# A hybrid decoder layer: own tokens scored as extra key columns, the first sample softmax between the prompt heads, a fused mask and maximum, stacked rotary scores

## The chip, the cores and the metric

One of the eight cores of a Trainium2 chip runs the whole kernel. A core has a matrix engine (TensorE, called PE in the profile), a vector engine (VectorE, DVE), a scalar engine for activations and copies (ScalarE, ACT), a general engine (GpSimd, POOL), and SyncE (SP), which here issues nearly all transfers to 16 DMA engines. They share the on-chip memory SBUF; PE writes its results to PSUM, eight banks of 512 fp32 numbers per partition. Each engine works through its own list of instructions in order and waits on semaphores for the others. The metric is the time of one execution in microseconds; lower is better.

## What is computed

One step of one decoder layer for a prompt of 256 tokens and for 8 sequences of 8 new tokens each, whose 1024 earlier tokens lie in a paged cache. In short:

```python
h = rmsnorm(x); z = h @ w_in                # q | latent c_kv | k_rope | pool input | 2 gates
# prompt: 16 heads, causal, 128 + 64 (rotary) dimensions
s = (q_nope @ k_nope.T + q_rope @ k_rope.T) * ATTN_SCALE
p = softmax(where(mask, s, -inf)); o = p @ v
# sample, per sequence: 1024 cached latents and 8 of its own tokens
q_lat = einsum('thd,rhd->thr', q_nope, w_uk)
s = (q_lat @ c_all.T + q_rope @ kr_all.T) * ATTN_SCALE     # 8 tokens x 16 heads = 128 rows
o_lat = softmax(where(mask, s, -inf)) @ c_all; o = o_lat @ w_uv
merged = sigmoid(gA) * (o @ w_attn_out) + sigmoid(gB) * (pooled @ w_pool_out)
x = x + merged @ w_o; x = x + conv_glu(rmsnorm(x)); y = rmsnorm(x)
```

Everything is fp32. The kernel gets near that precision with the faster format fp32r by splitting each operand in a high part (the value rounded to fp32r) and a low part (the rest), and adding high x high, high x low and low x high.

## The kernel before

The 320 tokens are the moving columns of nearly every product. The weights come in slabs of 128 x 2048 numbers (1 MB). For each slab SP issues the transfer into `w_raw`, ACT copies it to `w_hi` (L484), DVE subtracts to `w_lo` (L884) and PE forms the products (L1434); two buffers of each alternate. Every engine has its part of the program written out by hand, and semaphores with counted values tie them together (`hi_ready`, `lo_ready`, `slab_used`, `slab_taken`).

**Start.** ACT's own queue brings `vec` (the gains and other vectors) and the first tile of x (L549, L550); SP's queue brings the first slab in pieces and the other tiles of x.

**`uk` and `uv`.** Eight slabs give the keys `kT` and values `vv` of the prompt.

**Prompt heads.** A loop of 16 heads and three more steps. In step i, PE scores head i in fp32 (`qn` with `kT`, and for the rotary part `qr` with `kr_half`, a copy of the rotary key for even and odd heads in which the other half of the rows is zero), transposes the probabilities of head i - 2 (L1672) and applies those of head i - 3 to the values. DVE scales and masks the scores in one pass (L1185) and takes two row maxima (L1191, one per 128 queries), divides head i - 1 by its sum (L1196, L1200), and makes the low part of the output of head i - 4 (`o_lo`). ACT does the exponentials (L706), copies the turned probabilities (`pt`) and the outputs (`o_hi`). Between these stand the first pieces of the sample part: latent queries (PE steps 1 to 8), the splitting of the first cached pages into halves (ACT `w_hi`, `k_rope`; DVE `w_lo`, `k_rope`), and the scores of sequence 0 (PE steps 11 to 15) and the first of sequence 1 (step 17).

**Sample loop.** A sequence has two groups of four pages, q = 0 and 1. Its scores are two chunks of 512 columns in two PSUM banks, each of fourteen products: eight with the high keys, four with the low keys, two rotary. `new_scores` adds a third piece: the 8 x 8 = 64 own tokens of all sequences, in fp32, masked so that only the sequence's own 8 count. Then the maximum (DVE, L1240 to L1247), the exponentials (ACT, L749, L751), the division (DVE, L1258), the turn on PE (L1729, L1733), its copy to SBUF (`spt`), and the product with the token-major pages (`c_raw`). The order on PE for sequence i is: scores q = 0 of i, turn of i - 1, scores q = 1 of i, own scores of i, values of i - 1.

After this PE goes through the output projections and the feed-forward part, which the change leaves alone.

## Time and profile before

| | us |
|---|---|
| median of 3 runs | 1988.13 (1987.9 to 1988.9) |
| the profiled execution | 1988.56 |
| its span, first to last instruction | 1986.6 |
| PE busy | 1959.0 (99%) |
| DVE busy | 1092.2 (55%) |
| ACT busy | 761.2 (38%) |

The profile records one execution. PE is busy nearly throughout; a product shows a busy time longer than its distance from the next, since products overlap in the pipeline, so distances between starts are what a product costs. The granted clock of PE is 1.0 in almost every slice (1.0 is 2.4 GHz, 0.5 is 1.2 GHz). The sixteen heads run from 606 to about 671 us, the sample loop until 798.

### The profile page before, as it was taken

The page shows a single profiled execution, that of the slowest core. Times are in us where ns is not written, and L with a number is a line of the kernel's source. Part 1 is how long each engine was busy: PE and PEld are TensorE (multiplying, and loading weights), DVE is VectorE, ACT ScalarE, POOL GpSimd, SP SyncE. Part 2 cuts the span into 40 slices and gives each one's busy share as a digit, 9 for nine tenths or more (in the row PEclk, how much of TensorE's full clock was granted, in tenths as well). Part 3 has the DMA queues.
Part 4 walks back from the last instruction along what each step waited for, and adds up shares of the span by engine and source line. Part 5 has one row for each costly group of instructions (what it writes and reads, how often), then busy time and mean ns, then how long its engine had stood idle before and what let it go on. Part 6 is the DMA issues. An engine that isn't in the chain of part 4 may idle for free.

```text
span 1986.6 us, 33915 instructions
## 1 busy us (share of the span) xinstructions
PE 1959.0 (99%) x13368; PEld 1935.2 (97%) x13368; DVE 1092.2 (55%) x1469; ACT 761.2 (38%) x836; POOL 48.8 (2%) x188
## 2 busy tenths in 40 slices
PE   8999999999999899999999999999999999999997
PEld 8999999999998799999999999999999999999997
DVE  6865344333335764355556655555556555565656
ACT  5356542332246654233334232333323333333334
POOL 1002000000000000000000000000000000000000
PEclk9999999999999999999999999999999999999998
DMA  6444444444444487454444434344444444444443
GB/s 248 142 151 178 148 148 148 148 149 148 149 173 157 141 281 285 149 202 149 149 150 158 163 136 161 148 148 148 148 148 148 148 149 148 146 153 143 159 140 121
DMA packets 59878, 318.13 MB, mean 160 GB/s; under 512 B 6514, under 2 KB 6834, under 8 KB 27186
## 3 DMA queue, kind: packets, MB, share of 16 engines
q1 hardware_dynamic: 58882, 312.85, 44.5%
q10 hardware_dynamic: 944, 4.57, 0.6%
q8 instruction: 34, 0.56, 0.1%
q14 instruction: 18, 0.15, 0.0%
HBM read 313.08 MB, written 4.32 MB: 160 GB/s over the span
## 4 chain that ended last, share of the span: by engine, by line
PE 97%; DVE 1%; ACT 1%; DMA 1%; issue 0%; SPq 0%; DVEq 0%; ACTq 0%
PE ps L1434 96%; PE ps L1729 0%; DVE w_lo L884 0%; DMA xT<-in_x 0%; DVE y_gain L884 0%; DMA w_raw<-in_cache_t 0%; DVE neg_max L1191 0%; ACT w_hi L484 0%; DVE sm L1185 0%; ACT sm L706 0%; SPq L359 0%; DVE k_rope L884 0%; ACT qlat L484 0%; PE ps L1672 0%; ACT pt L484 0%
## 5 line engine op out<-in xcount | busy, mean ns | idle before, releaser
L884 DVE TENSOR_TENSOR w_lo<-w_raw,w_hi 128x2048 fp32r<-128x2048 f32 (+2 forms) x270 | 608.1, 2253 | 453.8 <-ACT w_hi L484 453.5
L1434 PE MATMUL ps<-h_hi,w_hi 128*128 128x320 f32 x2512 | 742.0, 308 | 9.1 <-ACT w_hi L484 9.1
L484 ACT ACTIVATE w_hi<-w_raw 128x2048 fp32r<-128x2048 f32 (+2 forms) x272 | 508.4, 1870 | 624.5 <-PE ps L1434 624.2
L1434 PE MATMUL ps<-h_lo,w_hi 128*128 128x320 f32 x2512 | 741.2, 309 | 0.0
L1434 PEld LDWEIGHTS ps<-h_hi,w_hi 128*128 128x128 f32 x2512 | 473.0, 188 | 9.6 <-ACT w_hi L484 9.1
L1434 PEld LDWEIGHTS ps<-h_lo,w_hi 128*128 128x128 f32 x2512 | 471.5, 188 | 0.5 <-DVE h_lo L985 0.3
L1434 PE MATMUL ps<-h_hi,w_lo 128*128 128x320 f32 x2496 | 391.1, 308 | 0.0
L1434 PEld LDWEIGHTS ps<-h_hi,w_lo 128*128 128x128 f32 x2496 | 372.5, 187 | 0.0
L1434 PE MATMUL ps<-hid_hi,w_hi 128*128 128x320 f32 x704 | 216.5, 308 | 0.0
L1434 PE MATMUL ps<-hid_lo,w_hi 128*128 128x320 f32 x704 | 216.5, 308 | 0.0
L1434 PE MATMUL ps<-hid_hi,w_lo 128*128 128x320 f32 x704 | 216.5, 307 | 0.0
L1434 PEld LDWEIGHTS ps<-hid_hi,w_hi 128*128 128x128 f32 x704 | 131.9, 187 | 0.0
L1434 PEld LDWEIGHTS ps<-hid_lo,w_hi 128*128 128x128 f32 x704 | 131.9, 187 | 0.0
L1434 PEld LDWEIGHTS ps<-hid_hi,w_lo 128*128 128x128 f32 x704 | 131.9, 187 | 0.0
L868 ACT ACTIVATE silu<-cv,vec 128x336 f32<-128x336 f32 x44 | 25.4, 577 | 213.0 <-DVE cv L1380 213.0
L884 DVE TENSOR_TENSOR x<-ps,x 128x320 f32<-128x320 f32 x176 | 80.3, 486 | 47.1 <-PE ps L1434 47.1
L1434 PE MATMUL ps<-o_hi,w_hi 128*128 128x320 f32 x256 | 75.4, 307 | 0.0
L1434 PE MATMUL ps<-o_lo,w_hi 128*128 128x320 f32 x256 | 75.3, 308 | 0.0
L1434 PE MATMUL ps<-m_lo,w_hi 128*128 128x320 f32 x256 | 75.3, 308 | 0.0
L1434 PE MATMUL ps<-m_hi,w_hi 128*128 128x320 f32 x256 | 75.3, 307 | 0.0
L1380 DVE SCALAR_TENSOR_TENSOR cv<-aext,vec,cv 128x336 f32<-128x336 f32 x88 | 50.1, 569 | 11.0 <-DVE cv L1377 0.2
L1434 PE MATMUL ps<-spt,c_raw 128*128 128x128 f32 x448 | 51.9, 276 | 0.0
(230 smaller groups left out, 1766.7 us busy)
## 6 DMA issues: line engine op xcount, KB each, us to landing
w_raw<-in_slabs SPq DMA_DIRECT2D x253, 1024.0 KB, 4.8
w_raw<-in_cache_t SPq DMA_DIRECT2D x64, 288.0 KB, 4.1
c_raw<-in_cache SPq DMA_DIRECT2D x56, 256.0 KB, 4.8
w_whole<-in_slabs SPq DMA_DIRECT2D x4, 1024.0 KB, 7.0
x_again<-in_x ACTq DMA_DIRECT2D x1, 2560.0 KB, 9.8
c_last<-in_cache SPq DMA_DIRECT2D x8, 256.0 KB, 4.2
xT<-in_x SPq DMA_DIRECT2D x3, 640.0 KB, 8.6
out_y<-y_gain SPq DMA_DIRECT2D x2, 640.0 KB, 3.1
```

Source lines behind the costliest of these rows:

```text
L484: return nc.scalar.activation(out, in_, ACT.Copy)
L868: nc.scalar.activation(silu[:, f % 2, CW - 1:], cv[:, 2, CW - 1:], ACT.Silu, bias=vec[:, bass.ds(c * FPC + (VEC["conv_b"] + f), 1)]).then_ ...
L884: return nc.vector.tensor_tensor(out, a, b, op)
L1380: nc.vector.scalar_tensor_tensor(out=dst, in0=src, scalar=w, in1=cv[:, j - 1, CW - 1:], op0=ALU.mult, op1=ALU.add).then_inc(cv_step, 1)
L1434: return nc.tensor.matmul(out, a, b, start=start, stop=stop, **kw)
```

## The change

1. **Own tokens as key columns.** The high and low keys of a sequence are now one tile each, `keys_hi` and `keys_lo`, of 4 x 1032 columns: 1024 cached and, behind them, the 8 own tokens of the sequence (`new_key_hi`, `new_key_lo`). The scores of sequences 1 to 7 are three chunks of 512, 256 and 264 columns, the last in PSUM bank 7. Sequence 0 keeps a separate piece, of 8 instead of 64 columns, in bank 6. The exponentials of sequences 1 to 7 are in three pieces, the maximum in one more.
2. **First softmax between the last heads.** The own scores of sequence 0 move to PE step 15, mask and maximum to DVE step 16, exponentials to ACT step 17, division to DVE step 18. On PE, the second group of sequence 1 comes whole before the first turn. Two key subtractions on DVE move from steps 7 and 8 to steps 9 and 11.
3. **Fused mask and maximum.** `tensor_tensor_reduce` adds the mask to the scores in PSUM, scales by -SCALE and takes the row minimum; it is built as two instructions per call, listed as ISA.
4. **Stacked rotary scores.** `q_stack` of each head holds the high part of its rotary query in 64 rows and the low part in the other 64; `k_stack` holds the high and the low part of the key in all 128. Two fp32r products replace an fp32 one. The stacks are made beside the `uk` and `uv` slabs; they lie in memory that the last sample buffers use later, so the token-major pages of sequence 0 are fetched after the last head's scores.
5. **Queues.** `vec` and the first tile of x are issued by SP, ahead of its other transfers; the page table comes later.

The core of the diff:

```diff
+CHUNKS = ((0, 4 * PAGE), (4 * PAGE, 6 * PAGE), (6 * PAGE, KEYS))
@@ SP
+            sp.dma_start(vec[:, :], vecs).then_inc(gain_in, 16)
+            x_tiles(0, 0, 1, x_first)
             sp.dma_start(*latent_rows(0, 0, 1)).then_inc(slab0_part[0], 16)
...
-            by_token(0, 1)
...
                 if i == -1:
+                    sp.wait_ge(sc_done, H)
+                    by_token(0, 1)
                     by_token(0, 0)
@@ ACT
-            act.dma_start(vec[:, :], vecs).then_inc(gain_in, 16)
-            act.dma_start(xT[:, 0:1, :], x[:, 0:1, :]).then_inc(x_first, 16)
...
+            def new_key_hi(b):
+                if b > 1:
+                    act.wait_ge(slab_used, GS + 2 * b)
+                copy(keys_hi[:, :, PAST:], new_columns(b))
+                copy(k_rope_all[:, PAST:], kr_new[:, b * NT:(b + 1) * NT]).then_inc(key_new_hi, 1)
...
+                if i == 16:
+                    new_key_hi(1)
                 if i == 17:
+                    exp_scores(0)
                     act.wait_ge(slab_used, GS + 2)
                     key_rope_hi(1, 1)
@@ DVE
-                    nc.vector.scalar_tensor_tensor(out=sm[:, i % 3, :], in0=ps[:, 2 + i % 2, 0:3 * P], scalar=SCALE,
-                                                   in1=const("mask", 3 * P), op0=ALU.mult, op1=ALU.add
-                                                   ).then_inc(sc_masked, 1)
-                    dve.wait_ge(sc_masked, i + 1)
                     for q in range(2):
                         c0, c1 = (0, P) if q == 0 else (P, 3 * P)
-                        nc.vector.tensor_reduce(nmx[:, 2 * i + q:2 * i + q + 1], sm[:, i % 3, c0:c1], AX.X, ALU.max,
-                                                negate=True).then_inc(mx_done, 1)
+                        nc.vector.tensor_tensor_reduce(sm[:, i % 3, c0:c1], ps[:, 2 + i % 2, c0:c1],
+                                                       const("mask", 3 * P)[:, c0:c1], -SCALE, -NEG, ALU.add, ALU.min,
+                                                       nmx[:, 2 * i + q:2 * i + q + 1]).then_inc(mx_done, 1)
...
                 if i == 7:
-                    dve.wait_ge(slab_used, G0["ukt"] + UKT_ORDER.index(2) + 1)
                     key_rope_lo(0, 0)
-                if i in (7, 8):
-                    key_lo(0, 0, i - 7)
+                if i == 9:
+                    dve.wait_ge(slab_used, GS)
+                    key_lo(0, 0, 0)
...
+                if i == 11:
+                    key_lo(0, 0, 1)
...
+                if i == 16:
+                    dve.wait_ge(slab_used, GS + 2)
+                    maximum(0)
@@ PE
-                        last = mm(out, qr[:, i // 2, q * P:q * P + P], kr_half[:, i % 2, 0:(q + 1) * P], False, True)
+                        for half in range(2):
+                            last = mm(out, q_stack[i][:, q * P:q * P + P], k_stack[:, half, 0:(q + 1) * P], False,
+                                      half == 1)
...
+                    if i == 15:
+                        pe.wait_ge(krn_lo, 1)
+                        new_scores()
...
+            def last_scores(b):
+                pe.wait_ge(spt_act, b)
+                pe.wait_ge(key_new_lo, b)
+                score_high(b, 2)
+                score_low(b, 2).then_inc(slab_used, 1)
...
                 if i == 1:
-                    score_low(i, 0)
+                    score_low(i, 0).then_inc(slab_used, 1)
                     score_high(i, 1)
+                    score_low(i, 1)
                     turn(b)
-                    score_low(i, 1)
...
-                new_scores(i)
+                last_scores(i)
```

On PE, the scores of one head before the change (`kT` and `qn` are the fp32 part without rotation, `kr_half` and `qr` the rotary part; an fp32 row here is issued as two instructions in the trace):

```order
L1434 MATMUL ps<-kT,qn 128x128
L1434 MATMUL ps<-kr_half,qr 128x128
L1434 MATMUL ps<-kT,qn 128x256
L1434 MATMUL ps<-kr_half,qr 128x256
L1672 MATMUL ps<-cst,sm 128x128 x3
```

and after it:

```order
L1546 MATMUL ps<-kT,qn 128x128
L1546 MATMUL ps<-k_stack,q_stack_138 128x128 x2
L1546 MATMUL ps<-kT,qn 128x256
L1546 MATMUL ps<-k_stack,q_stack_138 128x256 x2
L1788 MATMUL ps<-cst,sm 128x128 x3
```

Each rotary product became two of the same width in the faster format; the rest stands as it stood.

On PE, the hand-over from the heads to the sample loop, from the turn of sequence 0 to its values, before the change (`cst,s_probs` is the turn, `w_lo` and `k_rope` the low half of the scores of sequence 1, `c_111,qlat` and `kr_new` its own scores, `spt,c_raw` the values):

```order
L1729 MATMUL ps<-cst,s_probs 128x128 x8
L1733 MATMUL ps<-cst,s_probs 128x128
L1434 MATMUL ps<-w_lo_54,ql_hi 128x512 x4
L1434 MATMUL ps<-k_rope_68,q_rope_hi 128x512
L1434 MATMUL ps<-k_rope_68,q_rope_lo 128x512
L1434 MATMUL ps<-c_111,qlat 128x64 x4
L1434 MATMUL ps<-kr_new,q_rope_hi 128x64
L1434 MATMUL ps<-kr_new,q_rope_lo 128x64
L1434 MATMUL ps<-spt,c_raw_74 128x128 x16
```

and after it:

```order
L1546 MATMUL ps<-keys_lo,ql_hi 128x256 x4
L1546 MATMUL ps<-k_rope_all,q_rope_hi 128x256
L1546 MATMUL ps<-k_rope_all,q_rope_lo 128x256
L1838 MATMUL ps<-cst,s_probs 128x128 x8
L1842 MATMUL ps<-cst,s_probs 128x128
L1546 MATMUL ps<-keys_hi,ql_hi 128x264
L1546 MATMUL ps<-keys_hi,ql_lo 128x264
...
L1546 MATMUL ps<-keys_lo,ql_hi 128x264 x4
L1546 MATMUL ps<-k_rope_all,q_rope_hi 128x264
L1546 MATMUL ps<-k_rope_all,q_rope_lo 128x264
L1546 MATMUL ps<-spt,c_raw_75 128x128 x16
```

The low part of the second group now stands ahead of the turn, and behind the turn a chunk of 264 columns takes the place of the own scores.

On DVE, the same place: the end of the heads (`o_lo` are the low outputs of the heads, `sample_max` and `sample_sum` belong to the sample softmax), before:

```order
L884 TENSOR_TENSOR o_lo<-ps,o_hi 128x256
L884 TENSOR_TENSOR w_lo_53<-w_raw_49,w_hi_51 128x1024
L1225 MEMSET s_probs 128x64
L884 TENSOR_TENSOR new_score<-ps,new_mask 128x64
L1240 TENSOR_REDUCE sample_max<-ps 128x1
...
L884 TENSOR_TENSOR k_rope_68<-w_raw_50,k_rope_68 64x4x64 x2
L884 TENSOR_TENSOR w_lo_54<-w_raw_50,w_hi_52 128x2048
L884 TENSOR_TENSOR sample_sum<-sample_sum 128x1
L1256 RECIPROCAL sample_sum<-sample_sum 128x1
L1258 TENSOR_SCALAR s_probs<-s_probs,sample_sum 128x1088
```

and after:

```order
L1272 TENSOR_REDUCE sample_max<-ps 128x1
...
L952 TENSOR_TENSOR o_lo<-ps,o_hi 128x256
L952 TENSOR_TENSOR sample_sum<-sample_sum 128x1
L1290 RECIPROCAL sample_sum<-sample_sum 128x1
L1292 TENSOR_SCALAR s_probs<-s_probs,sample_sum 128x1088
L952 TENSOR_TENSOR keys_lo<-w_raw_49,keys_hi 128x2x4x128
L952 TENSOR_TENSOR o_lo<-ps,o_hi 128x256
L952 TENSOR_TENSOR ql_lo<-qlat,ql_hi 128x512
L952 TENSOR_TENSOR keys_lo<-c_112,keys_hi 128x4x8
L952 TENSOR_TENSOR k_rope_all<-w_raw_50,k_rope_all 64x4x64 x2
L952 TENSOR_TENSOR keys_lo<-w_raw_50,keys_hi 128x4x4x128
```

The softmax of sequence 0 moved up past the last outputs of the heads and past both remaining key subtractions.

## Rows read from the trace of the kernel before

**Rows 1.** PE's waits, whole span: waiter and releaser, us in total, times, longest.

```profile
PE ps L1729 <- DVE s_probs L1258: 1.6, 1, 1.6
```

**Rows 2.** The chain of waits, start: from us, for us, what.

```profile
1.20 6.73 DMA xT<-in_x
...
9.15 598.28 PE ps L1434 x4030
```

**Rows 3.** Timeline of ACT in the uk slabs: start, us, instruction, idle before.

```profile
578.09 1.91 ACT L484 ACTIVATE w_hi<-w_raw 128x2048 fp32r<-128x2048 f32 x1 [2.77 <-PE ps L1434]
```

**Rows 4.** Windows: busy us of PE, PEld, DVE, ACT, POOL; clock; DMA share, GB/s.

```profile
0.00:8.00 8.00, 0.00 (x0) 0.00 (x0) 0.06 (x1) 1.49 (x2) 0.20 (x4) 1.00 0.73 221
674.00:678.00 4.00, 4.00 (x14) 3.18 (x13) 3.41 (x10) 1.53 (x5) 0.00 (x0) 0.57 0.91 276
```

**Rows 5.** Transfers issued from 0 to 20 us: KB, us to landing.

```profile
vec<-in_vecs ACTq DMA_DIRECT2D x1, 134.0 KB, 5.5
```

**Rows 6.** Timeline of PE, one period of the sample loop.

```profile
729.86 0.48 PE L1434 MATMUL ps<-w_hi,ql_hi 128*128 128x512 f32 x1
...
733.20 1.00 PE L1434 MATMUL ps<-c,qlat 128*128 128x64 f32 x8
...
734.12 0.28 PE L1434 MATMUL ps<-kr_new,q_rope_lo 128*128 128x64 f32 x1
734.23 7.39 PE L1434 MATMUL ps<-spt,c_raw 128*128 128x128 f32 x64
...
745.62 1.04 PE L1729 MATMUL ps<-cst,s_probs 128*128 128x128 f32 x8
```

**Rows 7.** Timeline of PE in the uk slabs, 256 columns.

```profile
561.05 0.28 PE L1434 MATMUL ps<-c_lo,w_hi 128*128 128x256 f32 x1
561.17 0.28 PE L1434 MATMUL ps<-c_hi,w_hi 128*128 128x256 f32 x1
```

**Rows 8.** Timeline of DVE in the same period of the sample loop.

```profile
734.46 2.29 DVE L884 TENSOR_TENSOR w_lo<-w_raw,w_hi 128x2048 fp32r<-128x2048 f32 x1
...
742.76 0.79 DVE L1258 TENSOR_SCALAR s_probs<-s_probs,sample_sum 128x1088 f32<-128x1088 f32 x1
```

**Rows 9.** Window behind the last transfer of the period.

```profile
736.00:737.00 1.00, 1.00 (x12) 1.00 (x11) 1.00 (x3) 1.00 (x2) 0.00 (x0) 1.00 0.01 2
```

**Rows 10.** Timeline of PE in the heads: head 7, start of head 8.

```profile
631.43 0.59 PE L1434 MATMUL ps<-kr_half,qr 128*128 128x256 f32 x2
631.86 0.49 PE L1672 MATMUL ps<-cst,sm 128*128 128x128 f32 x3
...
634.58 0.44 PE L1434 MATMUL ps<-kT,qn 128*128 128x128 f32 x2
```

**Rows 11.** Timeline of PE at the hand-over.

```profile
674.16 1.86 PE L1434 MATMUL ps<-w_lo,ql_hi 128*128 128x512 f32 x4
...
684.24 7.39 PE L1434 MATMUL ps<-spt,c_raw 128*128 128x128 f32 x64
```

**Rows 12.** Timeline of DVE in step 8 and at the hand-over.

```profile
638.85 0.55 DVE L1185 SCALAR_TENSOR_TENSOR sm<-ps,cst 128x384 f32<-128x384 f32 x1
...
639.96 0.15 DVE L1196 RECIPROCAL row_inv<-row_sum 128x2 f32<-128x2 f32 x1
640.15 0.55 DVE L1200 TENSOR_SCALAR sm<-sm,row_inv 128x128 f32<-128x128 f32 x2
640.61 0.42 DVE L884 TENSOR_TENSOR o_lo<-ps,o_hi 128x256 fp32r<-128x256 f32 x1
...
676.47 0.85 DVE L884 TENSOR_TENSOR k_rope<-w_raw,k_rope 64x256 fp32r<-64x256 f32 x2
```

**Rows 13.** Timeline of ACT: key pieces in step 14, exponentials of sequence 0.

```profile
662.78 0.83 ACT L484 ACTIVATE k_rope<-w_raw 64x256 fp32r<-64x256 f32 x2
663.63 1.06 ACT L484 ACTIVATE w_hi<-w_raw 128x1024 fp32r<-128x1024 f32 x1
...
676.47 1.11 ACT L749 ACTIVATE s_probs<-ps,sample_max 128x1024 f32<-128x1024 f32 x1 [3.08 <-DVE sample_max L1247]
```

More of the change, by code:

```diff
@@ L662, in _, with stack_hi @@
             copy(kr_new[:, :], kr[:, NP:T]).then_inc(krn_hi, 1)
+            copy(k_stack[:, 0, :], kr[:, 0:NP]).then_inc(ks_hi, 1)
+            def stack_hi(n):
+                if STACK_FREE[n]:
+                    act.wait_ge(qst_lo, STACK_FREE[n])
+                h = STACK_ORDER[n]
+                rows = slice(64 * (h % 2), 64 * (h % 2) + 64)
+                copy(q_stack[h][rows, :], qr[rows, h // 2, 0:NP]).then_inc(qst_hi, 1)
             for j in range(4):
@@ L669, in _ @@
                 last.then_inc(slab_taken, 1)
+                for n in range(*STACKS_OF[j]):
+                    stack_hi(n)
             for j in range(4):
@@ L1165, in _, with stack_lo @@
             steps("q_nope", scaled("q_nope", qn), take_first=True)
-            for j in range(6):
-                split(G0["uk"] + 2 + j)
+            def stack_lo(n):
+                h = STACK_ORDER[n]
+                here, other = 64 * (h % 2), 64 * (1 - h % 2)
+                dve.wait_ge(qst_hi, n + 1)
+                tt(q_stack[h][other:other + 64, :], qr[here:here + 64, h // 2, 0:NP], q_stack[h][here:here + 64, :],
+                   ALU.subtract).then_inc(qst_lo, 1)
+            dve.wait_ge(ks_hi, 1)
+            tt(k_stack[:, 1, :], kr[:, 0:NP], k_stack[:, 0, :], ALU.subtract).then_inc(ks_lo, 1)
+            for j in range(8):
+                if j < 6:
+                    split(G0["uk"] + 2 + j)
+                for n in range(*STACKS_OF[j]):
+                    stack_lo(n)
             dve.wait_ge(qrs_hi, 1)
```

264 lines of the change are left out of this document (155 added, 109 removed).

## Prediction

> **What bounds the kernel now.** I read the views in this order: the waits of the matrix engine (TensorE, PE), the chain of waits, windows and timelines of the stretch from 604 to 800 us, then the transfers. PE waits for almost nothing: 9.1 us at the start and some 8 us in waits of under 2, the last of them 1.6 us for the probabilities at 680 [rows 1]; the chain is PE for 97% of the span. Two things follow. A matrix product taken away shortens the kernel as long as its neighbours keep up, and outside three places nothing else counts: the start (0 to 9.15 us) [rows 2], the sixteen prompt heads with the hand-over to the sample loop (606 to 684), and the sample loop (684 to 798). The change touches these three; what it does elsewhere (no zero-padded copies of the rotary key, two narrow copies per head beside the `uk` and `uv` slabs) lies under PE: a slab lasts 5.65 us there, and ScalarE (ACT) waits 2.77 of it for PE [rows 3], VectorE (DVE) for ACT; the change adds 0.4 us twice or three times on either. The last stacked query must be ready when PE begins the heads at 605.95; counted from the end of the third `uv` slab (600.5) through ACT's 1.1 us copy, two more 0.4 us copies and their 0.4 us subtractions it is ready at 603.3. If that cover of 2.6 us were gone it would cost what is missing, once.
>
> **The start.** The chain is the first tile of x, issued at 1.20 and landed at 7.93, then two ACT operations, then PE at 9.15 [rows 2]. The transfers moved 221 GB/s over the first 8 us, 1.8 MB [rows 4], while vec and that tile are 0.29 MB: they share the 16 DMA engines with what SyncE's queue (SP) has issued. Now they go first in SP's queue. What bounds the gain: vec, first in its queue, landed 5.5 us after its issue, and the same quick landing for the tile (1.20 + 5.5 = 6.7) gives 1.3 us [rows 2, 5]; that is my value, since every later piece was there before ACT took it. From above: if only 0.55 MB had to move before PE starts, it starts near 6.3, a gain of 2.8. From below: each slab piece is issued 2 x 0.45 us later and the interleaving cost nothing: a loss of 0.9. The Trainium skill (DMA: Bandwidth & Descriptors, Issuing engines are not separate DMA queues) says that spreading issues over engines saves only issue time, as all share the same 16 DMA engines, and (Queues, rings and completion order) that each engine takes turns between the queues; the late landing beside the other queue's 1.8 MB agrees. By the first rule alone the move would lose the 0.9.
>
> **One sequence of the sample loop.** A period is 16.66 us of back-to-back products: the turn of the probabilities ends at 729.86, fourteen 512-column products of the second half of the keys end at 733.20, the own tokens' scores (four fp32 products of 64 columns, issued as eight, and two more) take until 734.23, values and the next first half until the next turn at 745.62 [rows 6]. In the change the 512 + 64 columns become 256 + 264. A 512-column product costs 0.233 us (3.34 less 0.08 for the first, by fourteen), a 256-column one 0.1175 (561.05 to 561.17) [rows 7], so about 0.457 ns a column: 264 columns are 0.1205. New: 14 x 0.1175 + 14 x 0.1205 + 0.08 for the first = 3.41 us against 4.37. It saves 0.96 us.
> Six such periods (sequences 2 to 7) give 5.8 us; sequence 1 is in the hand-over. Do the others keep up? Counted from the end of the turn, DVE copies its half of the turned probabilities, subtracts the next keys from 734.46 (ACT's copy of them sets this), takes the maximum, splits the other half, and scales the probabilities until 743.5 [rows 8]: 13.7 us. The change adds a second reduction and a third partial sum, about 0.15, so 13.85, and the next turn then comes 14.7 us after the last: 0.85 us of slack is left of 2.1. The own key columns for the next sequence are made behind the scaling, in the shadow of 2 us. The transfers: page data issued after DVE's second subtraction land 20.7 us after the turn that began the period (ACT waits 0.4 us for them now), which is 5.0 us after the next turn instead of 4.0; ACT has them split at 7.8 and DVE wants them at 8.9. The last of the token-major pages have landed by 736.0 [rows 9], 22.6 after their period's turn (713.35), and are wanted at 22.6. So nothing takes PE's place, but barely. Bounds for this term: 2.9 (half is lost to these neighbours) and 6.1.
>
> **Heads and hand-over.** Per head the rotary score was an fp32 product of 128 and one of 256 columns, 0.22 and 0.43 us; it becomes two fp32r products each. 2 x 0.11 (the 0.11 of the 64-column product at 734.12 [rows 6]) saves nothing, 2 x 0.1175 for the 0.43 from 631.43 to 631.86 saves 0.20 [rows 7, 10]. Heads 0 to 7 are PE-bound (PE has no wait before 640): 8 x 0.2 = 1.6 us.
> From the scores of head 8 (634.58) to the first value product of sequence 0 (684.24) are 49.7 us [rows 10, 11]. Counting its instructions at full speed gives 39.0 us of PE work: eight score steps of 1.31, ten transposes of 0.33, eleven value steps of 0.6, latent queries 1.7, four score chunks of 512 columns 13.7 (high part 1.95, low part 1.48 each), own scores 1.1 and 1.0, turn 1.0. About 1.7 is lost to the granted clock: 0.57 in the window from 674, the lower of the two levels for most of it, after PE had been idle 1.75 us, and products take 0.43 instead of 0.233 [rows 4, 11]. The other 9.0 are waits, 4.9 in the heads, where the DVE is the chain.
> PE's work falls by 8 x 0.2 and by 0.96 for sequence 1: 36.4.
> The waits: DVE's scale-and-mask plus two maxima take 1.11 us from issue to issue (638.85 to 639.96) [rows 12]. Two fused instructions and two reads of the running result replace them; the trace shows neither. From below: two plain passes over the same widths, 0.46 us (640.15 to 640.61). From above: no gain, 1.11. I take 0.75, nearer to the plain passes, with a short read behind each; it frees 0.36 of DVE per head. More weighty is that the key subtractions (1.13 each) move from steps 7 and 8 to 9 and 11: DVE stood at step 7 until ACT's key copy was done at 636.8 and reached head 8 only at 638.85; it will at about 635.4. From then on DVE has 1.75 us per step and 6.6 us of inserted work, 20.6 in eight steps, PE 25.9: I walk through the steps and find PE short by only 1.2 us in all, and its last value step ends at 664.6 (now 671.3).
> What is late next is behind it. The sequence 0 softmax now stands between the heads: maximum on DVE done at 662.2, exponentials on ACT at 664.4 to 665.9, scaling at 667.0, not 680.7. But ACT's copy of the last head's output is queued behind the exponentials, the rotary part and a key half (1.11 and the short pieces behind it, 1.45; 0.83; 1.0) [rows 13], so DVE frees PE only at 668.5: a wait of 3.9. Then the second half of sequence 1's keys, split on ACT by 668.9 and on DVE from 670.3 to 673.4 (0.85 and 2.29 us, as from 676.47 now [rows 12, 8]), holds up its low part, which now stands ahead of the turn: 2.4. Then the last chunk waits for ACT's copy of the turned tile: 1.0. With 0.4 more for the fused instructions: 1.2 + 3.9 + 2.4 + 1.0 + 0.4 = 8.9. For the clock I keep 1.0 us, as PE again idles before the hand-over. New stretch 36.4 + 8.9 + 1.0 = 46.3 for 49.7: 3.4. With the 1.6 above: 5.0. Bounds: 1.9 (waits of 12) and 8.9 (waits of 6, no slow clock).
> The Trainium skill (TensorE: Matmul & The Clock Gate, Part 1) has the PE clock fall to half after idling and rise after sustained work. The trace agrees at 674 us. By this rule, applied to three waits instead of two, the low part, the turn and the last chunk (3.4 us) could all run at half rate and cost up to 3 us; this is the second rival below.
>
> **Sum.** 1.3 + 5.0 + 5.8 = 12.1 us. Against the profiled execution's 1988.56 (span 1986.6) that is 1976.5; the median of the runs is 0.4 lower, so 1976.0.
>
> **Rivals.**
> (1) The sample loop is held by DVE's chain. For it: slack falls from 2.1 to 0.85 and ACT, DVE and SP all hang on one another. Against it: each piece of it is a row and nothing in it gets longer. If the chain is 1.4 us longer than I count, a period gives 0.4 instead of 0.96: 3.4 us less, 1979.4.
> (2) The hand-over gives almost nothing: a slow clock through turn and last chunk (2 us more) and 1.5 us more waiting at the last key half. For it: the clock did this before at the same place; against it: PE has 2.5 us of continuous work before the critical part. 1979.5.
> (3) More than forecast: the start gives 2.8 and the hand-over waits 3 us less: 1971.5.
> (4) Slower: the split keys are written in runs of 128 elements with a stride, into one tile for both halves, instead of one run of 2048. If that made the copies and subtractions half as slow again, the chain turn, ACT copy 1.92, DVE 2.29, maximum, DVE 2.29, scaling would grow by 3.25 us to 17.1, the period to 18.0, and seven periods would lose 9.4 us, against 6.3 saved elsewhere at best: 1991. It makes the whole slower from 1.4 times on. Against it: the half pieces, whose reads skip columns already, take 1.06 on ACT against 1.91 for a contiguous slab [rows 13, 3], so strides have cost nothing so far.
> (5) The change does not do what it says: the fused instruction costs over 2 us per head, DVE becomes the bound of the heads and eats the rest: 1987 to 1989.
>
> **How the numbers follow.** Forecast 0.62, (1) 0.09, (2) 0.16, (3) 0.08, (4) 0.03, (5) 0.02. Range: from (3) with its own play, 1970.5, to (1) and (2) together, 1982.5; what is left out is (4), (5) and the tail of (3). A difference below 0.2% (4 us) is what a measurement of this kernel can't tell from none: faster 0.95, same 0.02, slower 0.03.
>
> **What would show it.** In the new profile: PE's first product near 7.8; rotary products spaced 0.117 at 256 columns; the loop's turns 15.7 us apart, with no PE wait between; the DVE's masked maximum near 0.75 us per head; the last value step of the heads near 663.3 (after the 1.3 us of the start); PE waiting for the last head's low part and for the second key half; the first value product of sequence 0 near 678. Turns 16.2 us or more apart, or a fused pair above 1.1 us, would make it wrong.

## The result, and the profile after

| | before | after |
|---|---|---|
| median of the runs | 1988.11 us (4 runs, 1987.9 to 1988.9) | 1974.2 us (4 runs, 1973.4 to 1974.7) |
| ratio | | 0.9929, 95% interval 0.9917 to 0.9941 |
| profiled execution | 1988.56 us, span 1986.6 | 1973.41 us, span 1971.6 |

The spans differ by 15.0 us. I cut both traces at instructions that they share and took the difference of the start times at each cut:

| stretch | forecast | gained |
|---|---|---|
| start to PE's first low run (before 16.99, after 15.61) | 1.3 | 1.38 |
| from there to the heads (605.95, 603.08): the same instructions | 0 | 1.49 |
| heads 0 to 7 (28.63, 27.05 us) | 1.6 | 1.58 |
| head 8 to the first value product (49.66, 45.95 us) | 3.4 | 3.71 |
| sample loop to the last values (8.16 to 12.28 ahead) | 5.8 | 4.12 |
| behind it: the same instructions | 0 | 2.73 |

PE's waits by line, whole span, in the profile after; of the columns the last three are us in total, times and longest. They answer to [rows 1]:

```profile
PE ps L1546 <- DVE o_lo L952: 3.9, 1, 3.9
PE ps L1546 <- ACT spt L527: 0.9, 1, 0.9
PE ps L1546 <- DMA c_raw<-in_cache: 0.8, 3, 0.3
PE ps L1546 <- DVE keys_lo L952: 0.7, 1, 0.7
```

The wait for the scaled probabilities is gone, as forecast. Waits for a head's low part, for the turned tile, for the second key half and for the token-major pages stand in its place; the last of these the forecast did not have.

PE's timeline at the start (start, us, instruction, idle before), for [rows 2]:

```profile
6.95 0.63 PE L1546 MATMUL ps<-h_hi,w_hi 128*128 128x320 f32 x1 [6.95 <-ACT w_hi L527]
7.38 0.47 PE L1546 MATMUL ps<-h_lo,w_hi 128*128 128x320 f32 x1
8.12 0.63 PE L1546 MATMUL ps<-h_hi,w_hi 128*128 128x320 f32 x1 [0.28 <-ACT h_hi L590]
...
13.95 0.47 PE L1546 MATMUL ps<-h_hi,w_hi 128*128 128x320 f32 x1
14.21 0.39 PE L1546 MATMUL ps<-h_lo,w_hi 128*128 128x320 f32 x1
14.44 0.31 PE L1546 MATMUL ps<-h_hi,w_hi 128*128 128x320 f32 x1
14.59 0.31 PE L1546 MATMUL ps<-h_lo,w_hi 128*128 128x320 f32 x1
```

PE starts 2.2 us earlier than before, then stands until 8.12 for the next tile of h. Until 14.2 its products are 0.267 us apart, which is the lower clock; from 14.44 on they are 0.147 apart.

DVE in the last head's step, with the fused instructions in the place of the three in [rows 12]:

```profile
654.72 0.29 DVE L1305 CUSTOM_DVE_ANT_0 sm<-ps,cst 128x128 f32<-128x128 f32 x1
654.94 0.08 DVE L1305 DVE_READ_ACCUMULATOR2_ANT neg_max<- 128x1 f32 x1
654.94 0.42 DVE L1305 CUSTOM_DVE_ANT_0 sm<-ps,cst 128x256 f32<-128x256 f32 x1
655.28 0.08 DVE L1305 DVE_READ_ACCUMULATOR2_ANT neg_max<- 128x1 f32 x1
655.28 0.16 DVE L1311 RECIPROCAL row_inv<-row_sum 128x2 f32<-128x2 f32 x1
```

Both together take 0.56 us from issue to issue (1.11 before).

The hand-over on ACT, DVE and PE, for [rows 11 and 13]. ACT does the exponentials (L760, L765), the rotary part, a key half and only then the last head's output; lines between are left out:

```profile
662.33 1.11 ACT L760 ACTIVATE s_probs<-ps,sample_max 128x1024 f32<-128x1024 f32 x1
...
663.42 0.35 ACT L765 ACTIVATE s_probs<-new_score,sample_max 128x64 f32<-128x64 f32 x1
...
663.75 0.83 ACT L527 ACTIVATE k_rope_all<-w_raw 64x256 fp32r<-64x256 f32 x2
...
664.59 1.06 ACT L527 ACTIVATE keys_hi<-w_raw 128x1024 fp32r<-128x1024 f32 x1
...
665.55 0.37 ACT L527 ACTIVATE o_hi<-ps 128x256 fp32r<-128x256 f32 x1
...
666.12 0.41 DVE L952 TENSOR_TENSOR o_lo<-ps,o_hi 128x256 fp32r<-128x256 f32 x1
...
666.79 2.04 PE L1546 MATMUL ps<-keys_lo,ql_hi 128*128 128x512 f32 x4 [3.94 <-DVE o_lo L952]
...
671.45 0.74 PE L1546 MATMUL ps<-keys_lo,ql_hi 128*128 128x256 f32 x4 [0.73 <-DVE keys_lo L952]
...
676.08 7.31 PE L1546 MATMUL ps<-spt,c_raw 128*128 128x128 f32 x64
```

In the loop, PE's value products of sequence 1, and then pieces of the chain of waits there (from us, for us, what). They answer to [rows 6]:

```profile
691.71 3.73 PE L1546 MATMUL ps<-spt,c_raw 128*128 128x128 f32 x32
695.62 3.84 PE L1546 MATMUL ps<-spt,c_raw 128*128 128x128 f32 x32 [0.17 <-DMA c_raw<-in_cache]
```

```profile
708.95 2.30 DVE keys_lo L952
714.37 1.37 SPq L416
721.93 5.70 DMA c_raw<-in_cache
727.68 7.99 PE ps L1546 x54
735.67 0.88 PE ps L1838 x8
```

The turns of sequences 1 to 6 come 16.07, 15.84, 16.22, 15.85 and 16.22 us apart (before 16.66; forecast 15.70). The chain no longer stays on PE: it goes from DVE's subtraction through SP's queue and a transfer of the token-major pages to the values.

### The profile page after: what moved, and what is told of

It reads as the page before. It is cut to its first block, busy times and chain, and to the rows that moved or that the text cites. A ratio compares the mean times of both kernels' runs of the same rounds, so it can differ in the third digit from the quotient of the medians.

```text
span 1971.6 us, 34072 instructions
## 1 busy us (share of the span) xinstructions
PE 1945.1 (99%) x13396; PEld 1928.0 (98%) x13396; DVE 1091.2 (55%) x1512; ACT 771.5 (39%) x881; POOL 46.9 (2%) x188
## 4 chain that ended last, share of the span: by engine, by line
PE 94%; SPq 1%; ACT 1%; DMA 1%; DVE 1%; issue 1%; DVEq 0%
PE ps L1546 94%; DMA c_raw<-in_cache 1%; SPq L416 1%; SPq L400 0%; DVE keys_lo L952 0%; ACT keys_hi L527 0%; DMA xT<-in_x 0%; DVE y_gain L952 0%; PE ps L1838 0%; PE ps L1788 0%; DVE k_rope_all L952 0%; ACT sm L782 0%; SPq L384 0%; ACT k_rope_all L527 0%; ACT pt L527 0%
## 5 line engine op out<-in xcount | busy, mean ns | idle before, releaser
L952 DVE TENSOR_TENSOR w_lo<-w_raw,w_hi 128x2048 fp32r<-128x2048 f32 (+1 forms) x251 | 571.0, 2275 | 446.4 <-ACT w_hi L527 446.3
L527 ACT ACTIVATE w_hi<-w_raw 128x2048 fp32r<-128x2048 f32 (+1 forms) x252 | 477.4, 1894 | 616.9 <-PE ps L1546 608.2
```

The lines of the kernel that those rows point to most:

```text
L527: return nc.scalar.activation(out, in_, ACT.Copy)
L952: return nc.vector.tensor_tensor(out, a, b, op)
```

## The experiments

The runs were measured in four groups, each together with the kernel before, and every ratio is to the kernel before of its own group. The changed kernel was measured a second time, 1974.66 us (5 runs, 1973.3 to 1975.1), in the group that holds the runs with the start, the fused instruction and the rotary stacks undone; the kernel before had a median of 1988.75 us there. It had 1988.38 in the group with the layout run and the first two new orders, 1987.99 in the one with the moved constants, both orders and the shifted activations, and 1988.42 beside the last run. Where two medians of different groups are compared, some 0.8 us can come from the group, and the difference by the ratios is given too.

**The changed kernel again** (no edit).

> The changed kernel once more, unchanged. Of the 15.0 us between the two profiled spans, 4.2 lie in stretches whose instructions are the same in both: 1.5 us between 60 and 603 us, nearly all of it in the uk and uv slabs, where a 256-column product came every 0.1135 us and not every 0.118, and 2.7 us behind 781 us, nearly all in the products of hid_hi and hid_lo. Theory P, the program sets this: the new profile shows 0.1135 us again, and start to first low run, heads and loop as before, the span within 0.5 us of 1971.6. Theory V, it varies from execution to execution: spacings of 0.118 are seen again and the span is 1 to 4 us longer, and the same stretches differ between the two profiles of one kernel.

Measured: 1974.66 us, ratio 0.9928 [0.9915, 0.9942], span 1971.7; from 20 to 676 us within 0.3 us of the first profile. The 256-column products are 0.1134 us apart in both. That is theory P. In the loop the turns came 16.34, 15.63, 16.50, 15.63 and 16.03 us apart, so the place of the long periods varies while the loop as a whole does not.

**The start undone.**

```diff
-            sp.dma_start(vec[:, :], vecs).then_inc(gain_in, 16)
-            x_tiles(0, 0, 1, x_first)
+            act.dma_start(vec[:, :], vecs).then_inc(gain_in, 16)
+            act.dma_start(xT[:, 0:1, :], x[:, 0:1, :]).then_inc(x_first, 16)
```

> The changed kernel with only vec and the first tile of x issued on ACT's queue again, as before. If the gain at the start is the order of the transfers alone, PE's first low run comes at 17.0 instead of 15.6 us, vec lands 5.5 and the tile 6.7 us after issue, and the whole is 1.4 us slower, about 1975.6. Rival: the two slab pieces that now come later in SP's queue had already cost something, so that the start comes back at 16.5 or earlier and the whole is under 1 us slower.

Measured: 1974.29 us (4 runs, 1972.3 to 1974.5), ratio 0.9924 [0.9909, 0.994]: no loss to be seen in the time, and not the 1.4. The numbers of the rival came true (under 1 us slower, the low run at 16.21); its reason, the later slab pieces, no run shows. In its profile vec landed 5.2 us and the tile 6.3 us after issue (2.7 and 3.6 after the change) and PE started at 8.73. Its timeline:

```profile
8.73 0.64 PE L1546 MATMUL ps<-h_hi,w_hi 128*128 128x320 f32 x1 [8.73 <-ACT w_hi L525]
...
14.20 0.42 PE L1546 MATMUL ps<-h_lo,w_hi 128*128 128x320 f32 x1
14.45 0.31 PE L1546 MATMUL ps<-h_hi,w_hi 128*128 128x320 f32 x1
...
16.21 1.04 PE L1546 MATMUL ps<-h_hi,w_lo 128*128 128x320 f32 x6
```

In this pair the clock rose at the same 14.4, though PE had started 1.8 us later, and the low run began 0.6 us later than after the change (15.61). Most of the head start went in the stand for the next tile and in products of 0.267 us.

The equal rise is chance. The products before the low run are the same in all fourteen profiles, yet the clock rose anywhere from 12.1 to 15.6 us, and the low run shifts with it. It began at 15.75 to 16.99 with these two transfers on ACT's queue (5 profiles, mean 16.3) and at 14.93 to 16.37 with them first on SP's (9 profiles, mean 15.7). Three other pairs, one profile of each order, have rises within 0.2 us of each other (13.4 and 13.2, 13.15 and 13.2, 15.2 and 15.1); in them the low run began 0.4, 0.3 and 0.25 us earlier with the transfers on SP. So at an equal clock the move is worth 0.3 to 0.6 us, less than what the moment of the rise adds or takes.

**The fused instruction undone.**

```diff
-                        nc.vector.tensor_tensor_reduce(sm[:, i % 3, c0:c1], ps[:, 2 + i % 2, c0:c1], ...)
+                    nc.vector.scalar_tensor_tensor(out=sm[:, i % 3, :], in0=ps[:, 2 + i % 2, 0:3 * P], ...)
+                        nc.vector.tensor_reduce(nmx[:, 2 * i + q:2 * i + q + 1], sm[:, i % 3, c0:c1], ...)
```

> The changed kernel with the mask and the maximum of the prompt heads as three instructions again (1.11 us from issue to issue against 0.56). DVE has 5.4 us idle in the 28 us from the scores of head 8 to the last value step. Theory A, part of that idle time takes it up: of the 8 x 0.55 = 4.4 us added there 1 to 2 come out on PE as waits for the normalised probabilities, the whole 1 to 2 us slower, about 1975.7. Theory B, DVE is the chain of these heads: over 3.5 us slower, 1978. Theory C, it is wholly hidden: within 0.3 us.

Measured: 1976.04 us, ratio 0.9937 [0.9922, 0.9953], 1.4 us over the changed kernel; from head 8 to the last value step 33.09 us and not 31.06. (The calls above are shortened; the exponential's sign and PE's wait for the masked scores went back with them.) Two of PE's waits from 600 to 680 us:

```profile
PE ps L1550 <- DVE o_lo L953: 3.9, 1, 3.9
PE ps L1792 <- DVE sm L1319: 1.4, 2, 1.1
```

This is theory A: the instruction is worth 1.4 us by the medians and 2.0 by the stretch of heads 8 to 15, where DVE's `sm` is waited for again.

**The rotary stacks undone** (one fp32 product per width, the zero-padded copies of the rotary key again, no stacked ones).

```diff
-                        for half in range(2):
-                            last = mm(out, q_stack[i][:, q * P:q * P + P], k_stack[:, half, 0:(q + 1) * P], False,
-                                      half == 1)
+                        last = mm(out, qr[:, i // 2, q * P:q * P + P], kr_half[:, i % 2, 0:(q + 1) * P], False, True)
```

> The changed kernel with the rotary scores of the prompt as one fp32 product per width again, and without the stacked copies on ACT and DVE. If PE is what bounds all sixteen heads, each step is 0.20 us longer (1.31 against 1.12 from the scores' start to the next step's transposes) and the whole 3.2 us slower, less up to 0.8 that waits for pt give back: 1976.6 to 1977.4. Rival: heads 8 to 15 are held by DVE and ACT, then only heads 0 to 7 count: 1.6 us slower, 1975.8. If the copies beside the uk slabs have to do with the quick 256-column products there, these are 0.118 us apart again and 0.9 us more is lost.

Measured: 1976.73 us, ratio 0.9941 [0.9926, 0.9956], 2.1 us over the changed kernel. Heads 0 to 7 took 28.63 us again (27.05): 1.58 us. Head 8 to the last value step took 31.84 (31.06): 0.78 us, where eight steps of 0.2 would be 1.6. So neither forecast of this run came true whole: PE sets the first half of the heads alone, and only half of the 1.6 comes out in the second. The 256-column products of the uk slabs stayed quick (0.1134), so the stacked copies beside them are not the reason.

**The kernel before again**, and its layout. The unchanged stretches had gained 4.2 us in every profile, so the question was what the change did to them. Beside the code it moved tiles: the low halves of the weight slabs begin 128 bytes, gain vectors and constants 256 bytes further up in each partition; the activations stayed.

> The kernel before once more, unchanged, for its profile. The stretches with the same instructions (the uk slabs, the products of hid) ran alike in five profiles of the changed kernel and its variants, and slower in the one profile of the kernel before. Theory P, the program sets this: the 256-column products of the uk slabs are 0.118 us apart again, and the span is within 0.7 us of 1986.6. Theory V, that one execution was a slow one: they are 0.1135 us apart and the span is 2 to 4 us shorter.

Measured: span 1986.4 (1986.6), 256-column products 0.118 us apart again, which is theory P.

```diff
-        w_hi = [sb(f"w_hi{s}", [P, SLAB], F32R) for s in range(2)]
-        lo_reg = [region(SLAB * 4) for s in range(2)]
+        hi_reg, lo_all = region(2 * SLAB * 4 + 128), region(2 * SLAB * 4 + 128)
+        w_hi = [sb(f"w_hi{s}", [P, SLAB], F32R, at=hi_reg + s * SLAB * 4) for s in range(2)]
+        lo_reg = [lo_all + s * SLAB * 4 for s in range(2)]
```

> The kernel before with nothing changed but where its tiles lie: the low halves of the weight slabs 128 bytes further up in each partition, the gain vectors and the constants 256 bytes, and the page numbers loaded later into the room of constants that are used up, as in the changed kernel. Theory L, the 4.2 us of unchanged stretches come from where the tiles lie: the 256-column products of the uk slabs are 0.1135 us apart, and the whole is 3 to 4.5 us faster than before (ratio 0.998). Theory N, they come from something else (the number or the place of the instructions): 0.118 us apart, no difference to before.

Measured: 1984.2 us (9 runs, 1982.6 to 1986.0), ratio 0.9977 [0.9967, 0.9987]. This is theory L: 4.2 us come from the place of tiles.

The next run leaves the low halves where they were and moves only the constants (a `region(256)` behind them):

> The kernel before with only the gain vectors and the constants 256 bytes further up and the page numbers loaded later, as in the layout run, but with the low halves of the weight slabs where they were. Theory L1, the place of the low halves (their start 128 bytes past a multiple of 256 before, on one in the changed kernel) makes the products of c and hid quicker: the 256-column products of the uk slabs are 0.118 us apart again and the time is that of before, 1988. Theory L2, the place of constants or the later page load does it: 0.1133 us apart and 1984.

Measured: 1988.34 us (10 runs), ratio 1.0002 [0.9992, 1.0011], which is theory L1: the two runs differ only in the place of the low halves. The same pair of product groups, twelve products apart, in the kernel before (again), with the constants moved, and with the low halves moved as well:

```profile
565.03 0.63 PE L1434 MATMUL ps<-c_hi,w_lo 128*128 128x256 f32 x4
566.44 0.63 PE L1434 MATMUL ps<-c_hi,w_lo 128*128 128x256 f32 x4
```

```profile
564.42 0.63 PE L1438 MATMUL ps<-c_hi,w_lo 128*128 128x256 f32 x4
565.83 0.63 PE L1438 MATMUL ps<-c_hi,w_lo 128*128 128x256 f32 x4
```

```profile
564.50 0.62 PE L1438 MATMUL ps<-c_hi,w_lo 128*128 128x256 f32 x4
565.86 0.62 PE L1438 MATMUL ps<-c_hi,w_lo 128*128 128x256 f32 x4
```

Twelve products took 1.41 us, 1.41 us and 1.36 us: 0.1178 and 0.1133 each.

**Earlier token pages in the loop** (on the changed kernel).

```diff
                 for q in range(2):
+                    if q == 1 and 1 <= i < NB - 1:
+                        by_token(i, q)
+                        del held[i, q]
                     if i + 2 < NB:
                         find_pages(i + 2, q)
...
-                    if i >= 1:
+                    if i >= 1 and (q == 0 or i == NB - 1):
```

> The changed kernel with the token-major pages of the second half of a sequence issued before SP waits for the second low split, and not behind the latent-major pages that this wait releases. The buffer is free 12.2 us after a turn, SP now issues at 14.4 + 2. If PE's waits for c_raw come from the place in SP's queue, all of them go, every period of the loop is 15.84 us and none 16.07 to 16.22: 0.8 to 1.2 us faster, 1973.6. Rival: the 16 transfer engines are the limit (0.81 busy in the loop); then the latent-major pages land as much later, ACT waits for them and PE for DVE: no gain, 1974.7, or a loss of up to 1 us.

Measured: 1972.24 us (5 runs, 1971.8 to 1972.5), ratio 0.9918 [0.9904, 0.9931], 2.4 us faster in the median (2.0 by the ratios), 1.3 in the span. The chain of waits in the loop is PE alone:

```profile
689.13 14.66 PE ps L1549 x114
703.78 0.91 PE ps L1841 x8
704.70 0.11 PE ps L1845
704.80 14.66 PE ps L1549 x114
719.46 0.88 PE ps L1841 x8
```

The turns come 15.64 to 15.75 us apart, less than the 15.84 expected, and from the first value product to the last turn it takes 99.46 us where the changed kernel took 101.23. That is 1.77 us less, where PE's listed waits had been 0.8. The weight loads had waited too (this row is of the changed kernel, from 676 to 781 us):

```profile
PEld ps L1546 <- DMA c_raw<-in_cache: 1.4, 3, 0.5
```

With the loop's 4.12 it makes 5.89. ACT now waits 15.4 us for its pages and not 6.0, but PE does not wait for it in the loop; the rival falls.

**Another order at the hand-over** (on the changed kernel): `o_hi` of the last head before the rotary part and both key halves on ACT, `o_lo` before the scaling on DVE, the second key half before the low part of a query.

```diff
                 if i == 17:
                     exp_scores(0)
+                if i == 18:
                     act.wait_ge(slab_used, GS + 2)
                     key_rope_hi(1, 1)
-                if i in (17, 18):
-                    key_hi(1, 1, i - 17)
+                    key_hi(1, 1, 0)
+                    key_hi(1, 1, 1)
...
                 if i == 18:
-                    normalise(0)
                     key_lo(1, 0, 1)
+                if i == 19:
+                    normalise(0)
```

> The changed kernel with another order at the hand-over on ACT and DVE: the copy and subtraction of the last head's output come before the rotary part and both key halves on ACT and before the scaling of the probabilities on DVE, and the second key half is subtracted ahead of the query's low part. Theory A, PE's wait of 3.9 us is only that place in the queues: PE resumes at 664.7 and not at 666.8, the wait for the second key half stays under 1.5 us since ACT's copy of it still ends at 666.9, and the first value product comes 2 us earlier, at 674; 1972.6. Theory B, ACT as a whole is what holds the hand-over: the wait moves to the second key half, and less than 0.7 us is gained.

Measured: 1973.53 us (5 runs, 1971.8 to 1975.0), ratio 0.9923 [0.9909, 0.9936]: 1.1 us under the changed kernel in the median (1.0 by the ratios), with runs too far apart to tell. The profiled run was one of the slower ones, 1974.60. PE's waits from 655 to 680 us:

```profile
PE ps L1549 <- DVE o_lo L953: 2.0, 1, 2.0
PE ps L1549 <- DVE keys_lo L953: 1.1, 1, 1.1
PE ps L1549 <- ACT spt L527: 0.9, 1, 0.9
PE ps L1549 <- ACT keys_hi L527: 0.4, 1, 0.4
```

The wait for the low part fell by 2.0 as in theory A, and those for the second key half grew by 0.8 in sum, within its bound. Yet from the last value step to the first value product it took 14.96 us, in the first profile of the changed kernel 14.89. PE's timeline behind the waits:

```profile
670.86 1.22 PE L1549 MATMUL ps<-keys_lo,ql_hi 128*128 128x256 f32 x4 [1.12 <-DVE keys_lo L953]
...
672.31 1.82 PE L1841 MATMUL ps<-cst,s_probs 128*128 128x128 f32 x8
```

The four products take 1.0 us to the next row's start where they take 0.58 in that profile, the turn 1.66 and not 0.88: the lower clock lasted until 673.9, where in that profile it ended at 669.7. That is the slow clock of my second rival, come true in this run. But the two profiles are no fair pair, since the clock's return varies with the old order too; the next run and the table behind it set that right.

**Both orders together.**

> The changed kernel with both new orders: token-major pages of the second half issued earlier, and the last head's output ahead of the exponentials' followers at the hand-over. The token pages alone gave 2.4 us (1972.2), the hand-over 2.0 us at its own wait, of which the next waits took back all but some 0.5. If they add up: 1971.5 to 1972.2, the turns 15.65 to 15.75 us apart. If the hand-over's gain comes through now that transfers do not hold the loop: 1970.5. Rival: the sequence-1 pages are what both compete for, then 1972.5 or more.

Measured: 1970.31 us (4 runs, 1970.0 to 1970.8), ratio 0.9909 [0.9893, 0.9926], span 1968.6: the 1970.5 of the case in which the gain at the hand-over comes through. It is 4.4 us under the changed kernel (3.8 by the ratios) and 1.9 under the token pages alone (1.8). Here the same stretch took 13.55 us, with the same waits for `o_lo` (2.0), `keys_lo` (1.1) and `spt` (0.9) but none for ACT's key half. The windows from 669 to 673 us (busy us of PE, PEld, DVE, ACT, POOL, then the clock) of this kernel, of the hand-over order alone, and of the changed kernel in its first and its second profile:

```profile
669.00:673.00 4.00, 2.05 (x16) 1.72 (x15) 2.54 (x4) 0.79 (x3) 0.00 (x0) 0.98 0.93 297
```

```profile
669.00:673.00 4.00, 2.88 (x14) 2.59 (x14) 2.51 (x3) 0.00 (x0) 0.00 (x0) 0.50 0.91 299
```

```profile
669.00:673.00 4.00, 3.27 (x23) 2.90 (x22) 2.38 (x2) 0.00 (x0) 0.00 (x0) 0.91 0.69 224
```

```profile
669.00:673.00 4.00, 3.95 (x21) 3.56 (x20) 2.29 (x1) 0.00 (x0) 0.00 (x0) 0.62 0.68 221
```

The profiles of the changed kernel and of its variants, by the moment at which the lower clock ended (S is from the last value step of the heads to the first value product):

| profiles | clock back, us | turn begins, us | S, us |
|---|---|---|---|
| old order: changed, fused undone, shifted activations | 669.7, 672.0, 670.9 | 672.3, 674.5, 672.5 | 14.87 to 14.89 |
| old order: changed again, start undone, stacks undone, token pages | 672.0, 673.2, 674.9, 672.6 | 672.5, 673.4, 675.0, 672.9 | 15.18 to 15.45 |
| new order: both orders | 669.2 | 671.0 | 13.55 |
| new order: hand-over alone, both orders with aligned high halves | 673.9, 673.9 | 672.3, 672.4 | 14.96, 14.93 |

Like with like, the new order is worth 1.3 us where the clock is back well before the turn, and 0.2 to 0.5 us where it is not. Each order met both cases. What decides when it is back was not tried. Nor does the earlier issue of the token pages decide it: the last profile of the table has it and its clock came back late.

**Where tiles lie: two more.** With all activations 64 bytes further up, modulo 256 (on the changed kernel):

> The changed kernel with every activation tile (h, c, hid, o, m and the rest) starting on a multiple of 256 bytes in its partition, where they now start 192 past one; two small tiles lie in used-up constants to make room. All else is unchanged. Theory M, a product streams more quickly when its operands start on such a multiple: the 320-column products of h, 0.1467 us apart now, come closer to 0.1417 (the 17 bytes in 16 columns that the quick 256-column ones show over their count) and the whole is 20 to 60 us faster. Theory N, only the low halves' place matters, or how it stands to the others: within 3 us of 1974.7, either way, with changes only in the uk, uv and hid products.

Measured: 1976.53 us, ratio 0.9942 [0.9925, 0.9958], 1.9 us slower (2.8 by the ratios). (The "17 bytes in 16 columns" of the text stands for 17 clock periods per 16 columns: at 2.4 GHz a 256-column product of 0.1133 us takes 272.) Products of h stayed at 0.1467. Theory M falls; the changes are in the products of c and hid, as in theory N. And with the high halves moved too (on both orders together):

> The run with both new orders, with the high halves of the weight slabs also starting on a multiple of 256 bytes, as the low halves do since the change (128 bytes past one so far); the activations keep their place, 192 past one. Theory D, the two halves of a slab must stand differently: with both alike, as they were before the change, the products of uk, uv and hid fall back to 0.118, 0.2333 and 0.1467 us and the whole is 4 us slower, 1974.5. Theory M, each half that starts on a multiple helps: 0.1133, 0.2311 and 0.1455 us or less, 1970.3 or up to 4 us faster. Theory R, what counts is how a weight half stands to the moving operand, which the run with the shifted activations also moved: anything in between, with some kinds of products quicker and others slower.

Measured: 1975.12 us, ratio 0.9935 [0.9921, 0.9948], 4.8 us slower than its base (5.2 by the ratios). Of the 4.7 us between the two profiles 2.3 lie in the hid products; most of the rest lies at the start and at the hand-over, where the clock stayed low through the turn. The time is near theory D's 1974.5, but for another reason: uk and uv did not fall back. All layouts, as the start of a tile modulo 256 bytes, and us per product (over 30 or more back to back):

| high, low, activations | uk, 256 | uv, 512 | hid, 320 |
|---|---|---|---|
| 128, 128, 192 (before, and constants moved) | 0.1178 | 0.2333 | 0.1467 |
| 128, 0, 192 (changed; layout run) | 0.1133 | 0.2311 | 0.1456 |
| 128, 0, 0 | 0.1185 | 0.2290 | 0.1467 |
| 0, 0, 192 | 0.1133 | 0.2289 | 0.1467 |

The rows fit neither "a start on a multiple is quicker" (hid is slow in the last row) nor "the halves must differ" (uk and uv are quick there). Theory R is what is left, and it names no rule. The hid products carry most: 2112 of them by 0.0011 us are 2.3 us; the c products of uk and uv carry 1.0.

Taken pair by pair, much of the gain of hid sits at the low halves. Between the constants run and the layout run, the step from a `hid_lo,w_hi` product to the `hid_hi,w_lo` behind it fell from 0.1466 to 0.1437 us and the next from 0.1467 to 0.1451, while the third, between two products of `w_hi`, rose from 0.1467 to 0.1479. The products of h show the first of these too (from `h_lo,w_hi` to `h_hi,w_lo`, 0.1473 to 0.1438), but 155 times and not 704, as their low products stand in long runs; their mean stays the same to 0.0001 us.

## Why the prediction was right or wrong

1976.0 was forecast and 1974.2 measured, inside the range and nearest to the likeliest case. The sum was made of right and wrong terms, which partly cancelled: the changed parts gave 10.8 us where I had 12.1, and the unchanged ones 4.2 where I had nothing. That it came out within 1.8 us is therefore partly luck; without the 4.2 it would have been 1978.4. No run undoes the own tokens as key columns or the earlier first softmax by themselves: what is said of them rests on the rows of the profile.

**The start, 1.3.** Measured 1.38 in the pair of profiles, but that is luck: undone, the run is no slower, over all profiles the step is worth some 0.6 us with a scatter of over 1 us within either order, and at an equal clock 0.3 to 0.6. The landing times came as forecast, even better (vec 2.7, tile 3.6 us after issue). What failed is "every later piece was there before ACT took it": PE started 2.2 us earlier and stood for the next tiles. The other thing the sum left out is the clock: what of the head start is left is spent in products of 0.267 us. The Trainium skill (TensorE: Matmul & The Clock Gate, Part 1) has the clock rise after sustained work; the traces agree in that it is low at PE's first product and up later, at a moment that moved by 3.5 us between the profiles. The other rule weighed there, of the Trainium skill (DMA: Bandwidth & Descriptors, Issuing engines are not separate DMA queues), has it that issuing from several engines saves only issue time. By landing times the place in the queue mattered (vec 5.2 and 2.7 us); by the time of the whole it could not be told.

**Heads and hand-over, 5.0.** Measured 5.29: 1.58 for 1.6 in heads 0 to 7, and 45.95 us for 46.3 in the stretch behind. The near match of the second hides errors that cancel. The fused pair took 0.56 us, nearer to my lower bound of 0.46 than to my 0.75. Of the waits, 3.9 for the last head's low part came as 3.94, 1.0 for the turned tile as 0.85, 1.2 in the heads as 0.8. The 2.4 for the second key half came as 0.73: ACT had split it by 666.9 and not 668.9, since the whole softmax was 2 us earlier (1.5 of it from the unchanged stretch ahead of the heads). In all PE stood 6.3 us and not 8.9. The lower clock took about 1.5 us and not 1.0, since the low part from 666.79 to 669.5 ran at it entirely (0.43 us a product). That leaves 38.1 us of work where I had 36.4. The kernel before has the same error: I called 9.0 us of its 49.7 waits, as what was left over after counting instructions, but PE's idle time before its products is 6.3 us there (3.2 in the heads, 3.1 behind). So my count of the work was too small in both kernels, by 2.7 and by 1.7, and most of that cancelled in the difference. What the uncounted time is stays open. Two pieces of the difference were sized wrongly as well: the rotary products of heads 8 to 15 are worth 0.78 and not 1.6, and the fused instruction, which I had as 0.4 of waiting and no gain of its own, costs 2.0 us of this stretch when it is undone.

The second rival, which rested on the clock, did not come in the first profile: turn and last chunk ran at 0.11 to 0.12 us a product. In the second profile of the same kernel the clock was back only at 672.0, just before the turn, and the stretch behind the heads took 0.3 us more; with the new order a late clock took 1.4. So it was a risk of this place, of a smaller size than the rival's 2 us.

**The loop, 5.8.** This is the mis-sized term: 4.12. The 3.41 us from turn's end to values was right (3.43 measured), and the first rival, DVE's chain, was not the limit. It was the transfers, of which I had written "nothing takes PE's place, but barely": pages landed 22.6 us after their turn and were wanted at 22.6. Even that reading was half a us too kind. I took the landing from a quiet window that began at 736.0; in the kernel before the last of the four pages was issued at 730.87 and landed 5.6 us later, 23.1 after the turn, and in the changed kernel the page of the chain landed 23.2 after its own. Three periods of five lasted 16.07 to 16.22 and the other two 15.84, where 15.70 was forecast. My own sign of being wrong, turns 16.2 us or more apart, was met by two of them, and "no PE wait between" failed. The bound of 2.9 held for this case; the value should have been put between. With the pages issued some 3.5 us earlier the period was 15.67 and the term 5.9. So the arithmetic of PE stands, and the queue order of SP was the price.

**What stood in no term.** 4.2 us come from the low halves' place. It is the line `hi_reg, lo_all = region(RT * KEYS * 4), region(RT * KEYS * 4)`: regions of 16512 bytes where two slabs of 8192 stood. I read it as room for eight more columns. The layout run against the constants run shows it; why the place matters is open.

## What to carry to other kernels

When a forecast finds that data arrive exactly when they are wanted, half the gain is at risk: look in the queue for a transfer that waits behind an unrelated one, and issue it as soon as its buffer is free. Take the landing of a transfer from its own row, not from a window in which traffic has ceased. Cut both traces at common instructions before explaining anything; a gain in a stretch that did not change may be as large as a term of the sum, and a kernel with only its tiles moved tells what it is. Before two profiles are compared, see whether the clock rose or came back at the same place in both. An earlier first product is worth its time only if the rest follows at once.

## What the hardware showed beyond that

- 128 bytes in where one operand starts changed fp32r products by 0.8% (320 columns of hid, 0.1467 to 0.1456 us) to 4% (256 columns of c, 0.1178 to 0.1133). The mean of the products of h hardly moved (0.1467 and 0.1466). Also products whose own two operands had not moved became quicker (`c_hi,w_hi`), when only `w_lo` had.
- With the same products at the start, the clock rose at 12.1 to 15.6 us in fourteen profiles; at the hand-over it came back at 669.7 or 672.0 in two profiles of one kernel, and with another order before the turn or only at its end.
- Masking with a running minimum in one instruction took 0.29 us for 128 columns and 0.42 for 256 from PSUM, with 0.08 us to read the result; the two pairs took half the time of mask and two maxima.
- With 0.81 to 0.87 of the transfer engines busy, four 256 KB pages of token-major data took 5.7 to 6.2 us from the last issue to landing in the loop, and stood on the chain three times.
